# Three weight casts, two low parts and two row loads of the output projection, placed ahead of the last gate half of stage B

## What is computed

```python
for l in range(DEPTH):                       # DEPTH = 2
    h = _rmsnorm(x, norm1_g[l])
    z = h @ w_in[l]
    mq, mk, mv, mi, mf, mo, aq, ak, av = jnp.split(z, split_idx, axis=-1)
    qk = jax.nn.silu(_causal_dwconv(jnp.concatenate([mq, mk], axis=-1), conv_w[l], conv_b[l]))
    hm = _mlstm_chunkwise(...)               # 4 heads of 128, a matrix memory
    hm = _rmsnorm(hm, ...) * jax.nn.sigmoid(mo)
    ha = _swa_sinks(_rope(...), _rope(...), av, sinks[l])   # 8 heads of 64, windowed
    x = x + jnp.concatenate([hm, ha], axis=-1) @ w_out[l]   # the output projection
    h2 = _rmsnorm(x, norm2_g[l])
    x = x + jnp.square(jax.nn.relu(h2 @ w_ff1[l])) @ w_ff2[l]
```

## Time and profile before

| | us |
|---|---|
| median of 3 runs (2163.51 to 2165.97) | 2165.57 |
| span of the profiled execution | 2163.3 |
| PE busy in it | 2106.8 (97%) |
| DVE busy | 1397.2 (65%) |
| ACT busy | 856.4 (40%) |
| POOL busy | 964.2 (45%) |
| PE's waits for low parts of the output projection, both layers | 7.4 |

### The profile page before, as it was taken

The page is one execution under the profiler, slowest core; times in us unless marked ns, Lnnn a source line. Parts: engine busy times, 40 slices in busy tenths (PEclk is TensorE's granted clock), DMA queues, the critical chain, the costliest instruction groups (busy, mean ns, idle before and its releaser), DMA issues.

```text
span 2163.3 us, 32423 instructions
## 1 busy us (share of the span) xinstructions
PE 2106.8 (97%) x10964; PEld 1752.3 (81%) x10964; DVE 1397.2 (65%) x1676; ACT 856.4 (40%) x1435; POOL 964.2 (45%) x701
## 2 busy tenths in 40 slices
PE   7999999999999999999999999999999999999998
PEld 7888877888788878888888887788878888788886
DVE  5037876477777787676630488654767777867664
ACT  5134443255666632121241343432666666322120
POOL 4235514324555456464541455134155445556552
PEclk9999999999999999999999999999999999999999
DMA  5222235416667789767442223344257766996763
GB/s 211 88 102 71 79 115 186 167 44 218 238 232 250 262 338 352 291 250 293 175 135 88 91 79 116 132 152 146 98 184 254 257 236 234 381 349 258 279 246 146
DMA packets 222799, 423.11 MB, mean 196 GB/s; under 512 B 24296, under 2 KB 158184, under 8 KB 214512
## 3 DMA queue, kind: packets, MB, share of 16 engines
q1 hardware_dynamic: 153664, 346.82, 45.1%
q10 hardware_dynamic: 69040, 75.05, 9.9%
HBM read 268.60 MB, written 153.22 MB: 195 GB/s over the span
## 4 chain that ended last, share of the span: by engine, by line
PE 74%; DVE 11%; issue 7%; ACT 5%; POOL 1%; DMA 1%; ACTq 0%; DVEq 0%; SPq 0%; POOLq 0%
PE ps L1805 27%; PE ps L1527 10%; PE ps L1457 10%; PE ps L1756 9%; PE ps L1617 7%; PE ps L1437 4%; DVE uf L2212 3%; ACT w1s L1037 2%; ACT uf L1051 2%; PE ps L1428 1%; DVE wo L2085 1%; PE ps L1551 1%; DVE uf L2282 1%; DVE sS L2230 1%; ACT uf L1053 1%
## 5 line engine op out<-in xcount | busy, mean ns | idle before, releaser
L1805 PE MATMUL ps<-w2s,uk 128*128 128x512 f32 x2688 | 612.9, 390 | 5.4 <-DMA uk<-uD 2.9
L1805 PEld LDWEIGHTS ps<-w2s,uk 128*128 128x128 f32 x2688 | 503.2, 188 | 114.3 <-issue 4.5
L2322 DVE TENSOR_TENSOR xs<-ps,xs 128x1024 f32<-128x1024 f32 x208 | 253.9, 1221 | 180.8 <-PE ps L1805 178.4
L1756 PE MATMUL ps<-hT,w1s 128*128 128x512 f32 x1344 | 317.6, 392 | 5.9 <-DVE uf L2282 3.2
L1756 PEld LDWEIGHTS ps<-hT,w1s 128*128 128x128 f32 x1344 | 250.3, 188 | 68.0 <-DVE uf L2282 12.6
L1379 POOL TENSOR_TENSOR w2s<-raw,w2s 128x1024 fp32r<-128x1024 f32 x64 | 188.4, 2957 | 248.6 <-ACT w2s L1149 248.6
L1375 POOL TENSOR_TENSOR w1s<-rawf,w1s 128x512 fp32r<-128x512 f32 x112 | 151.3, 1360 | 216.2 <-ACT w1s L1037 216.2
L1527 PE MATMUL ps<-hT,whi 128*128 128x512 f32 x768 | 244.0, 399 | 0.0
L1756 PE MATMUL ps<-tT,w1s 128*128 128x512 f32 x1008 | 237.3, 389 | 0.0
L1756 PEld LDWEIGHTS ps<-tT,w1s 128*128 128x128 f32 x1008 | 189.1, 188 | 39.4
L1457 PE MATMUL ps<-ahi,hT 128*128 128x512 f32 (+1 forms) x768 | 213.0, 361 | 3.3 <-DVE hT L1853 3.3
(11 more groups left out here) (216 smaller groups left out, 3105.0 us busy)
## 6 DMA issues: line engine op xcount, KB each, us to landing
uk<-uD SPq DMA_DIRECT2D x64, 1024.0 KB, 7.8
raw<-in_wstream SPq DMA_DIRECT2D x100, 512.0 KB, 5.9
uk<-uD SPq DMA_DIRECT2D x64, 768.0 KB, 5.9
rawf<-in_wstream SPq DMA_DIRECT2D x64, 512.0 KB, 4.3
uD<-uh ACTq DMA_DIRECT2D x64, 512.0 KB, 6.3
uD<-uf SPq DMA_DIRECT2D x64, 512.0 KB, 7.6
uD<-uh ACTq DMA_DIRECT2D x64, 384.0 KB, 4.2
uD<-uf SPq DMA_DIRECT2D x64, 384.0 KB, 6.8
```

The lines of the kernel that those rows point to most:

```text
L1756: mm = pe.matmul(ps[:, bank, :], w, x[:, k, :], start=(first and k == 0 and i == 0), stop=(k == 3 and i == 2), skip_group_check=True)
L1805: mm = pe.matmul(ps[:, bank + tp, :], u, w2s[r][:, w, k, :], start=(r in (1, 2, 5) and k == 0 and i == 0), stop=(k == 1 and i == 2), skip_ ...
L2322: V.tensor_tensor(y, ps[:, bank:bank + 2, :], y, ALU.add).then_inc(y_acc, 1)
```

## The change

ACT makes `split_out(0)` to `split_out(2)` ahead of `tanh_gate(5)`, and `split_out(3)` behind it, ahead of `squares(0, 0)`. DVE makes `lo_out(0)` and `lo_out(1)` ahead of `gate(5)`; `lo_out(2)` and `lo_out(3)` take the places that those had in the first `step_c`. SP issues `unit_c(6)` and `unit_c(7)` ahead of the store of the second gate half. PE gets one wait more ahead of the first block, for ACT's `tanh_gate(5)`, which has to have read the PSUM bank that the block writes. Nothing is computed that was not computed before, and nothing is left out.

```diff
@@ SP, load_b
+                def unit_c(k):
+                    out_split(sp, l, k - 6)
+                    sp.dma_start(out_raw(k), wstream[l, UB + ROW[k]]).then_inc(s_raw[k - 5], 16)
                 def load_b(j, last):
...
                     for x in range(2):
+                        if last and x == 1:
+                            unit_c(6); unit_c(7)
                         sp.wait_ge(b_gs, (l * 4 + j) * 2 + (x + 1))
                         alone(sp)
                         sp.dma_start(gD[j, :, x * 512:(x + 1) * 512], acc[x][:]).then_inc(b_go[x], 16)
...
                 load_gate(0, 0, True)
                 load_kv(0, 1, True)
-                unit_c(6)
                 sp.dma_start(xt[0][:], res_t[0]).then_inc(c_xt[0], 16)
-                unit_c(7)
                 load_gate(0, 1, True)
@@ ACT, step_b
                     if last:
                         decays(0, 0, True)
                         att_hi(0, 0)
+                        split_out(0); split_out(1); split_out(2)
                     tanh_gate(5)
...
-                split_out(0); split_out(1)
+                split_out(3)
                 squares(0, 0)
-                split_out(2)
                 decays(0, 1, False)
-                for k in range(3, 8):
+                for k in range(4, 8):
                     split_out(k)
@@ PE, step_c
                         scores_c(0, 1, 1, T + 1)
+                        pe.wait_ge(b_ev, (l + 1) * 24 + 2)
                         pe.wait_ge(c_al, T + 1)
@@ DVE, step_b
                     if last:
                         first_chunk()
+                        lo_out(0); lo_out(1)
                     gate(5)
@@ DVE, step_c
                     if first:
-                        lo_out(0)
+                        lo_out(2)
...
                     if first:
-                        lo_out(1)
+                        lo_out(3)
...
-                    if first:
-                        lo_out(2); lo_out(3)
```

More of the change, by code:

```diff
@@ L540, in load_x @@
                         sp.dma_start(out_t[i - 3], xs[:, i - 3, :]).then_inc(s_spill, 16)
-                def unit_c(k):
-                    out_split(sp, l, k - 6)
-                    sp.dma_start(out_raw(k), wstream[l, UB + ROW[k]]).then_inc(s_raw[k - 5], 16)
                 for b in range(2):
@@ L955, in att_hi @@
                     nc.scalar.copy(mxh[p][:, 0:4, :], att[p][:]).then_inc(c_ah, 1)
[L957 to L960, removed]
                 def split_out(k):
@@ L968, in split_out @@
                     nc.scalar.copy(woh[ROW[k]], out_raw(k)).then_inc(w_hi, 1)
+                step_b(0, False)
+                with act.Fori(1, MH - 1) as j:
+                    step_b(j, False)
+                step_b(MH - 1, True)
                 def squares(j, p):
@@ L1958, in weights, with lo_out @@
                         V.tensor_copy(kTs[:], qkT[:, i + 1, MH:2 * MH, :]).then_inc(c_ks, 1)
+                def lo_out(k):
+                    dve.wait_ge(w_hi, l * U + (UA + UB + k + 1))
+                    V.tensor_tensor(wol[ROW[k]], out_raw(k), woh[ROW[k]].bitcast(F32), ALU.subtract).then_inc(c_wl, 1)
                 def first_chunk():
@@ L2080, in _ @@
                 dve.wait_ge(c_one, l * 3 + 3)
-                def lo_out(k):
-                    dve.wait_ge(w_hi, l * U + (UA + UB + k + 1))
-                    V.tensor_tensor(wol[ROW[k]], out_raw(k), woh[ROW[k]].bitcast(F32), ALU.subtract).then_inc(c_wl, 1)
                 def step_c(j, p, first, last):
```

## The result

The changed kernel takes 2170.05 us (median of 18 runs, 2166.55 to 2172.42). The kernel before, in 18 runs on the same chips, takes 2165.72 (2161.99 to 2168.78). The ratio is 1.0019, 95% interval 1.0013 to 1.0026: **slower by 4.3 us**, outside the predicted range and on the side of the third rival.

The account below looks back on a forecast made before the run. PE, busy 97% of the span, was taken as the bound, with 7.4 us of waits. Per layer -0.87 + 0.3, say -0.55, two layers -1.1, took 2165.57 to 2164.5 us; range 2161.3 to 2167.8.

Parts of the forecast that it names:

- the third rival: xt's landing passes 329.9; at 330.9 mixf is 1.0 us late per layer, low clock 1.1 more: 2169.8, chance 0.13.
- The casts: ACT ahead of the last tanh: casts fit into 3.00 us of idle time; at worst tanh comes 0.1 us later.
- The low parts and gate(5): DVE: two low parts of 1.22 us ahead of gate(5) make it 0.85 us late.
- PE's gap: PE's first two blocks no longer wait; its fourth block ends at about 325, 4.3 us earlier.
- hn: POOL's low part of block 4 holds up fsc; hn ends at 326.5, mixf could start at 327.1 by PE and DVE.
- The store: SP: second gate half's store, behind 1 MB of loads, lands at 321.7; tile 0's gate is issued at 321.9, 2.0 us late.
- my late bound: The store follows all of block 7 plus half a load's 1.3 us, landing at 322.3.
- From the gate's issue to xt's landing: SP's queue: xt lands 7.1 us after the gate's issue, at 329.0, so mixf starts at 329.05, 0.87 us gained per layer.
- The clock: PE's idle piece before mixf may bring the 1.2 GHz level: 0 to 1.1 us per layer, taken as 0.3.
- The cover that I counted on: Behind mixf, DVE's own waits set the second tile's hn, hiding 0.8 us of a low-clock stretch of some 1.9 us.
- The first two rivals: Stage C: loads don't delay the store, 2161.5, chance 0.16; or xt doesn't matter and hn decides, 2160.0, chance 0.06.
- The fourth: Later waits absorb the change's effect: within 0.2 us of before, 2165.5, chance 0.05.

Follow-up runs that it names:

- own_sem_behind: The changed kernel with the two row loads right behind the gate's store and mixf waiting for the gate alone (own semaphore); 2160.62 us, ratio 0.9971.
- the fill: The changed kernel plus 18 idle PE matmuls behind the first tile's transposes of hn; 2169.09 us, ratio 1.0017 to the kernel before.
- loads_back: The changed kernel with the two row loads back in their old places, casts and low parts still moved; 2168.74 us, ratio 1.0016.
- gate_own_sem: The changed kernel with gate and xt on two semaphores, so mixf waits for the gate and not xt; 2162.75 us, ratio 0.9984.
- one_load_ahead: The changed kernel with one row load ahead of the gate's store and the other right behind it; 2166.04 us, ratio 1.0001.
- loads_behind_store: The changed kernel with both row loads issued right behind the store of the second gate half; 2163.64 us, ratio 0.9992.

## Why the prediction was wrong

By its own steps, with after's times set back by the 0.86 us:

- **The casts**: right. Three in 2.94 us, and the tanh starts at 316.51, where it was 316.50.
- **The low parts and gate(5)**: right in kind, a little dear. gate(5) starts at 317.79, 0.65 us late in place of 0.85, and the second half's store goes at 318.37 (forecast 318.55).
- **PE's gap**: right. The fourth block ends at 324.67 (forecast about 325), and no block waits for a low part.
- **hn**: right in mechanism. POOL's low part of block 4 holds fsc, which takes 2.38 us. But POOL's instruction began 1.05 us earlier than I put it, so hn starts at 325.29 in place of 326.5. By PE and DVE alone mixf would start at about 326.7; own_sem_behind shows it, 13.86 us after gate(4).
- **The store**: here the prediction failed. The term that was mis-sized is the landing of the loads ahead of the store. I had the store land 3.15 us after its issue, and at most 3.75. It took 5.4 us in layer 0 and 5.1 in layer 1. My late bound had the right form: it put the store half a load's transfer, 0.65 us, behind block 7, and the store did land 0.6 to 0.7 us behind block 7 in both layers. But block 7 landed at 323.1, where I had 321.6. I had made that up from a pair of loads of another stage, with 3.5 us for the first and 1.3 us of transfer. Here the two loads took 4.6 and 5.2 us in layer 0, 3.4 and 4.9 in layer 1, and 1.7 and 2.6 us lay between their landings. A further 0.6 us I lost by taking 321.7 in place of my own late bound, 322.3. So the gate was issued at 323.92 and not near 321.9. The Trainium skill (DMA: Bandwidth & Descriptors, Queues, rings and completion order) says that each engine takes a queue's descriptors in ring order; the three landings behind none, one and two loads (2.1, 3.7, 5.4 us) agree.
- **From the gate's issue to xt's landing**: right, 7.0 us (forecast 7.1). With the store's true time in my own chain, mixf comes out at 318.37 + 5.4 + 0.2 + 7.1 = 331.1; it started at 330.98. So all of the miss up to mixf, 1.9 us in layer 0 and 1.5 in layer 1, is the store's.
- **The clock**: mis-sized. I took 0.3 us per layer and allowed 1.1; from first to second mixf 1.5 and 1.0 us were lost in the trace, and the fill gave the same places back. No run shows the 1.9 us that I put a whole low stretch at; the earlier trace rows give 0.8 us for 24 matmuls behind one. Here the low level held for 10.2 us in layer 0 and 6.8 in layer 1. The cover that I counted on was DVE's own chain, 0.8 us; it was used up, and the chain of waits then ran through PE and no longer through DVE. What this costs in whole time stays open, as said above.
- **The rivals**: the third one was the case in its mechanism (xt's landing passes 329.9) and its place. Its size, forecast 2169.8 and measured 2170.05, is in part luck. It had mixf at 330.9, by a gate issued at 322.5 and 8.4 us from there to xt; mixf came at 330.98, by a gate issued at 323.92 and 7.0 us from there. Two errors of 1.4 us cancel. I gave this rival 0.13, because I held the store's late bound to be an extreme. That was too little: what the trace of before did not show, 1 MB ahead of a small store, I had priced with transfers that had the queue to themselves. The first two rivals are out: the store is held up, and xt does matter. The fourth, that later waits absorb it all, is out as well, since the interval of the ratio lies above 1.

What I did not see at all is that the loads' old place had its own price once PE's gap was closed (loads_back). The two edits on ACT and DVE win time once mixf no longer waits for xt (gate_own_sem, 3.2 us under the kernel before), and by the medians most with the loads right behind the store as well (own_sem_behind, 5.6 us), where the store lands after 2.1 us and the copy behind mixf takes 0.23 us, in place of the 1.49 in loads_back.

## What to carry to other kernels

A load that is moved earlier in an issue queue is also moved ahead of everything that it passes. Look for the small transfer that somebody waits for round trip (a store that must land before it is read back), and price its landing as that of the last transfer now ahead of it and a little more (0.6 to 0.7 us here). When a stall is closed, the waits that had been hidden by it become the bound: list what else the next instruction waits for, and give a transfer that it doesn't read a semaphore of its own.

## What the runs showed of the hardware

- A store of 256 KB landed 2.0 to 2.1 us after its issue with no load just ahead of it in SP's queue; behind one or two loads of 512 KB it landed 0.6 to 0.7 us after the last of them, 3.0 to 5.4 us after its own issue (the change and one_load_ahead, both layers).
- Two loads of 512 KB issued 1.1 us apart, ahead of the store, took 4.6 and 5.2 us to land in layer 0 and 3.4 and 4.9 in layer 1; in layer 0, issued 0.4 us apart they took 4.1 and 5.0 (loads_behind_store), and a pair in the MLP stage 3.5 and 4.4. While the first pair ran in layer 0, the DMAs moved only 180 to 209 GB/s in two of the 1 us stretches (320 to 322). Why the same bytes are slower here was not found.

```profile
320.00:321.00 1.00, 1.00 (x7) 1.00 1.18 209
321.00:322.00 1.00, 1.00 (x6) 1.00 0.54 180
```

- Two operations of 128x4 on DVE that started while POOL made a low part ended with it: 2.38 us for fsc and 1.49 us for a copy (in loads_back) that takes 0.16 in the trace of the change. The SBUF page of the Trainium skill (SBUF — State Buffer, Who interferes with whom) tells of a port pair that DVE and GpSimd share, and that whoever issues first holds it; these two durations agree.
- Closing four short waits of PE (0.27 to 1.66 us each in layer 0) and leaving one of 5.04 us dropped the granted clock to 0.50 where it had been 1.00 in the same stretch, and 18 matmuls in that wait brought it back to 1.00. A long wait is not needed for it: two waits of 1.36 and 0.79 us brought the low level in layer 0 of own_sem_behind and not in layer 1. What decides between these two the traces don't show.
